# A two-model transformer kernel: GpSimd makes the output weights' remainders, and half of the attention rows are transposed during the last heads

## The chip, the cores and the metric

One Trainium2 chip, one core of it (NeuronCore). The metric is the device time of one launch in microseconds (us), the median of several executions. Engines: TensorE (PE) multiplies and transposes matrices, VectorE (DVE) and ScalarE (ACT) work on rows, GpSimd (POOL) is a third engine for rows and for gathers, SyncE (SP) issues the loads.

## The reference

256 rows of 1024 go first through two layers of a first model (attention, pooling, then an expert layer that gathers rows of two tables), then through four layers of a second one, and it is these four that the change touches. Cut to what matters:

```python
for i in range(4):                       # mixers: diff, moba, swa, diff
    a = rms_norm_2(h, attn_norm_g[i])
    h = h + mixer(a)                     # in-projection, attention, @ w_out
    h = h + sqrelu_mlp(rms_norm_2(h, mlp_norm_g[i]), mlp_w_up[i], mlp_w_down[i])

# inside diff_attention: 8 heads of 128 columns, each from two score matrices
p = softmax(s); p = p[:, :, 0] - lam * p[:, :, 1]
o = einsum('bhqk,bkhe->bqhe', p, v)
o = rms_norm_2(o, sub_g) * (1.0 - lambda_init)   # a norm per row and head
return o.reshape(B, S, H * DIFF_V_DIM) @ w_out
```

The moba and swa mixers have 16 heads of 64 columns and no norm per head.

## The kernel before, in words

All of it is written by hand: each engine has its own program, and semaphores are the only tie between them, so the order of the source is the order on each engine. 256 rows are NT = 2 tiles of 128.

**Matrix products in the last layers.** A product is made in three passes of reduced-precision matmuls (`three`, L773): high part by high part, remainder by high part, high part by remainder. A weight block of 1024 x 512 (a unit) is loaded by SP into one of two ring slots; ACT writes the high part of each of its four pieces (`high_at`, L1495, the instruction is L1502), and DVE the remainder, raw minus high (`low_at`, L1702, instruction L1706, 128x1024). SP loads unit u only when the remainders of unit u - 2 are made. The left operand is treated alike: PE transposes a group of four 128x128 blocks into a psum bank (`tr_group`, L712), ACT copies it to `xT_high` (`xT_high`, L1519; instructions L1523 without and L1526 with gains), DVE makes `xT_low` (`xT_low`, L1746; L1751 and L1755). `linear2` (L1122) then multiplies piece by piece; piece p needs the remainders of weight piece p and the p-th group of the left operand.

**Attention** (`attention`, one function per engine: PE L809, ACT L1325, DVE L1772) is a software pipeline over steps i = 0 to nsub + 3, nsub = 16. In step i, PE makes scores i (L826), transposes the probabilities of a head (L836) and multiplies an older head with the values (`values`, L848, L858). ACT takes exponentials (L1350) and copies transposed probabilities (L1332). DVE adds the mask to the scores (L1784), takes reciprocals of the sums (L1829) and copies finished heads, scaled, to `tokb` (`heads`, L1820). With the diff mixer two score matrices make one head: DVE combines them (`probs`, L1836 and L1842), and it sums each head's squares (`head_squares`, L1809).

**The end of attention and the output projection**, the place of the change. The high pieces of the first output unit (o0) are made by ACT within attention, in steps 5, 7, 9, 12 (diff), 5 to 8 (moba) or 13, 15, 16, 17 (swa). Their remainders are made by DVE in steps 16 to 18 (`after`, L2339), between the copies of the last heads. Then, once all heads are copied, the diff mixer takes means and reciprocals of the squares (L2363, L2364), ACT takes the square root (L1572; its table is loaded at L1570), and DVE scales both row tiles, 128x1024 each (L2370). For every mixer DVE then signals `tok_ready`, PE transposes groups 0 and 1 of `tokb` into psT, ACT and DVE split them, and `linear2` of o0 begins; groups 2 and 3 are transposed after its pieces 0 and 1.

**GpSimd** has nothing to do in the last four layers. In the two first layers it makes one remainder in four (L2429), which shows what such an instruction takes there.

## Time and profile before

| | us |
|---|---|
| median of 3 runs (3406.3 to 3417.52) | 3413.79 |
| the profiled execution's own time | 3393.41 |
| its span | 3391.3 |
| PE busy in the span | 2414.8 |
| DVE busy | 2118.6 |
| POOL busy | 1014.6 |
| ACT busy | 937.3 |

The four last layers begin at about 2127 us. There PE is busy in nine tenths of nearly every slice, DVE in five or six tenths, ACT in four or five, POOL in none. The profile names the line of kernel.py with L, and PEld is the load of a matmul's stationary operand. Rows give start and duration in us, the engine, line and operation, what was written and read, and in brackets how long the engine sat idle before and what released it. "x8" are eight like instructions merged in one row.

### The profile page before, as it was taken

To read this page: it belongs to the slowest core of one execution; us is meant where nothing else is said; L and a number is where in the kernel's file an instruction comes from. 1 tells how busy PE (TensorE), PEld (TensorE's weight loads), DVE (VectorE), ACT (ScalarE), POOL (GpSimd) and SP (SyncE) were. 2 spreads that over 40 slices of the span, in tenths; PEclk is the share of its full clock that TensorE was granted. 3 is DMA by queue.
4 is the path that set the end of the run, shared out by engine and by line. 5 is a ranking of instruction groups with operands and counts; after the bars stand their busy time and mean duration, and the time that the engine had idled before them with its cause. 6 is when DMAs were issued, how large, how long until landed. Compare 5 with 4: busy or idle time off the path is not lost.

```text
span 3391.3 us, 35250 instructions
## 1 busy us (share of the span) xinstructions
PE 2414.8 (71%) x12383; PEld 1718.0 (51%) x12383; DVE 2118.6 (62%) x4448; ACT 937.3 (28%) x1486; POOL 1014.6 (30%) x1044
## 2 busy tenths in 40 slices
PE   4996455444433998444545533889999999999898
PEld 3755222122101865221212200669888987997797
DVE  6965765666654975766656664565555556556654
ACT  2411110011101510101100100554455445545543
POOL 0202656666664200566666665000000000000000
PEclk9998776676766998666677755989999998999899
DMA  8764999999998872999998999525543542555243
GB/s 317 283 225 152 390 372 356 385 384 344 351 380 321 297 273 82 362 396 366 379 376 343 343 370 374 180 92 176 196 149 125 187 147 100 183 191 174 100 177 132
DMA packets 311815, 892.92 MB, mean 263 GB/s; under 512 B 22424, under 2 KB 31616, under 8 KB 311552
## 3 DMA queue, kind: packets, MB, share of 16 engines
q0 software_dynamic: 147456, 536.94, 41.1%
q1 hardware_dynamic: 164224, 354.32, 29.4%
q8 instruction: 68, 1.11, 0.1%
q14 instruction: 67, 0.55, 0.0%
HBM read 890.13 MB, written 1.05 MB: 263 GB/s over the span
## 4 chain that ended last, share of the span: by engine, by line
PE 50%; issue 14%; DVE 11%; POOL 10%; another core or an unknown queue 8%; DMA 4%; ACT 2%; SPq 0%; DVEq 0%; POOLq 0%; ACTq 0%; PEld 0%
PE lin L776 8%; PE lin L777 8%; PE lin L778 8%; PE psS L1020 4%; POOL proj L2445 4%; PE lin L1064 3%; PE lin L746 3%; POOL ring L2458 3%; DVE proj L2145 2%; POOL vbuf L2458 2%; PE psT L778 2%; PE psT L777 2%; PE psS L777 2%; PE psS L778 2%
## 5 line engine op out<-in xcount | busy, mean ns | idle before, releaser
L2145 DVE CUSTOM_DVE_ANT_0 proj<-proj,psT 128x1024 f32<-128x1024 f32 x512 | 608.2, 1219 | 228.8 <-DMA proj<-in_expert_u,eidx 145.6
L1706 DVE TENSOR_TENSOR weights_split<-ring,weights_split 128x1024 fp32r<-128x1024 f32 (+1 forms) x376 | 450.7, 1208 | 375.9 <-ACT weights_split L1502 373.0
L2445 POOL DMA_INDIRECT proj<-in_expert_u,eidx x512 | 483.5, 944 | 506.1 <-DVEq L2119 318.1
L1502 ACT ACTIVATE weights_split<-ring 128x1024 fp32r<-128x1024 f32 (+1 forms) x376 | 391.5, 1046 | 467.5 <-PE lin L778 291.4
L1064 PE MATMUL lin<-ring,rowb 128*32 128x512 f32 x896 | 205.0, 813 | 254.9 <-DMA pr<-in_expert_v,pT 103.6
L1064 PE MATMUL lin<-vbuf,rowb 128*32 128x512 f32 x1024 | 214.4, 830 | 195.4 <-issue 100.5
L776 PE MATMUL lin<-weights_split,xT_high 128*128 128x512 f32 (+1 forms) x736 | 297.0, 404 | 11.3 <-DVE xT_low L1755 5.2
L2458 POOL DMA_INDIRECT vbuf<-in_expert_v,pT x256 | 240.9, 941 | 165.1 <-issue 75.6
L778 PE MATMUL lin<-weights_split,xT_high 128*128 128x512 f32 (+1 forms) x736 | 288.9, 392 | 0.0
L1020 PE MATMUL psS<-xT,ring 128*128 128x256 f32 x1024 | 260.7, 414 | 31.1 <-issue 24.9
L2458 POOL DMA_INDIRECT ring<-in_expert_v,pT x224 | 215.3, 961 | 190.1 <-remote 72.5
L1020 PEld LDWEIGHTS psS<-xT,ring 128*128 128x128 f32 x1024 | 210.4, 209 | 104.7 <-issue 69.6
L1445 ACT ACTIVATE gel<-hdot 128x16 f32<-128x16 f32 x32 | 6.9, 216 | 839.8 <-remote 311.9
L1064 PEld LDWEIGHTS lin<-ring,rowb 128*32 128x32 f32 x896 | 37.0, 131 | 381.3 <-issue 198.7
L1064 PEld LDWEIGHTS lin<-vbuf,rowb 128*32 128x32 f32 x1024 | 42.2, 139 | 322.7 <-issue 320.1
L776 PE MATMUL lin<-weights_split,act_split 128*128 128x512 f32 x512 | 200.1, 391 | 0.0
L777 PE MATMUL lin<-weights_split,act_split 128*128 128x512 f32 x512 | 199.5, 390 | 0.0
L778 PE MATMUL lin<-weights_split,act_split 128*128 128x512 f32 x512 | 199.2, 389 | 0.0
L777 PE MATMUL lin<-weights_split,xT_low 128*128 128x512 f32 (+1 forms) x480 | 187.0, 390 | 0.0
L1051 PE MATMUL psS<-const,pT 128*128 128x16 f32 x64 | 16.6, 337 | 238.9 <-DVE pT L2132 135.6
L1430 ACT ACTIVATE sm<-psS 128x512 f32<-128x512 f32 x32 | 19.1, 597 | 550.2 <-remote 277.8
L776 PEld LDWEIGHTS lin<-weights_split,xT_high 128*128 128x128 f32 x736 | 143.3, 195 | 45.1 <-issue 9.4
(279 smaller groups left out, 4950.9 us busy)
## 6 DMA issues: line engine op xcount, KB each, us to landing
ring<-in_mlp_w_up SPq DMA_DIRECT2D x32, 2048.0 KB
ring<-in_mlp_w_down SPq DMA_DIRECT2D x32, 2048.0 KB
ring<-in_w_in SPq DMA_DIRECT2D x16, 2048.0 KB, 16.3
ring<-in_w_query SPq DMA_DIRECT2D x16, 2048.0 KB
vbuf<-in_ada_w SPq DMA_DIRECT2D x12, 2048.0 KB, 11.9
ring<-in_diff_w_in SPq DMA_DIRECT2D x12, 2048.0 KB, 13.1
ring<-in_ada_w SPq DMA_DIRECT2D x8, 2048.0 KB, 15.1
ring<-in_moba_w_in SPq DMA_DIRECT2D x6, 2048.0 KB
```

The costliest lines, as they stand in the source:

```text
L746: mm = pe.matmul(lin[:, pair + t, :], lhs[:, k, t * P:(t + 1) * P], rhs[:, k, :], start=(k == 0), stop=(k == kc - 1))
L776: pe.matmul(out_ap, lhs[0], rhs[0], start=first, stop=False, skip_group_check=True)
L777: pe.matmul(out_ap, lhs[1], rhs[0], start=False, stop=False, skip_group_check=True)
L778: return pe.matmul(out_ap, lhs[0], rhs[1], start=False, stop=last, skip_group_check=True)
L1020: mm = pe.matmul(psS[:, 1, (b % 2) * S:(b % 2 + 1) * S], ring[:, j, k, b * P:(b + 1) * P], xT[:, k, :], start=(k == 0), stop=(k == KC - 1))
L1064: mm = pe.matmul(lin[32 * b:32 * b + 32, 2 * half + t, :], wst[:, cb % 2, 4 * b + s, :], vrow(SETROWS * s + b)[:, half * 512:(half + 1) * ...
L1430: act.activation(qTx[:, lo:lo + 2, :].rearrange("p a s -> p (a s)"), psS[:, 1, :], ACT.Copy).then_inc(q_used, 1)
L1502: act.activation(part(p, 0, kind, w), raw_piece(slot, p, kind, w), ACT.Copy).then_inc(hi_ready, 1)
L1706: dve.tensor_tensor(part(p, 1, kind, w), raw_piece(slot, p, kind, w), part(p, 0, kind, w).bitcast(F32), ALU.subtract).then_inc(lo_ready, 1)
L2145: dve.tensor_tensor_reduce(ubuf[:, n % GB, :], ubuf[:, n % GB, :], x_row, 1.0, 0.0, ALU.mult, ALU.add, hdot[:, cb, k:k + 1]).then_inc(h_re ...
L2445: pool.indirect_dma_start(out=ubuf[:, (16 * cb + k) % GB, :], out_offset=None, in_=table["u"], in_offset=bass.IndirectOffsetOnAxis(ap=eidx ...
L2458: pool.indirect_dma_start(out=vrow(SETROWS * s + b), out_offset=None, in_=table["v"], in_offset=bass.IndirectOffsetOnAxis(ap=eidxT[:, cb % ...
```

## The change

Four things, in the last four layers only.

1. The four remainders of unit o0 are made by GpSimd, in each of the four layers (16 instructions), each as soon as ACT's high piece is there. DVE makes none of them any more.
2. PE transposes groups 0 and 1 (heads 0 to 3 with diff, 0 to 7 with moba and swa) in step 18 of attention, before it multiplies the last heads, into banks 2 and 3 of `lin`. It waits for `tok_ready` there, which DVE now signals twice per layer, the first time at the start of step 17.
3. With diff, mean, reciprocal, square root and scaling are done per half of the heads: the first half's statistics in step 16 and its scaling at the start of step 17; the second half's scaling after the split of groups 0 and 1. ACT loads the square root's table in step 16, ahead of its last copy.
4. ACT and DVE split groups 0 and 1 from `lin` right after attention.

```diff
@@ PE, attention(..., early=None) @@
                         mm.then_inc(pt_done, 1)
+                    if early is not None and i == m.nsub + 2:
+                        early()
                     o = m.head_at(i, 3)
@@ PE, per layer @@
+                def first_heads():
+                    pe.wait_ge(tok_ready, 2 * i + 1)
+                    pe.wait_ge(lin_used, C.lin)
+                    for g in range(2):
+                        for n, (b, t) in enumerate((b, t) for b in range(2) for t in range(NT)):
+                            mm = pe.transpose(lin[:, 2 + g, n * P:(n + 1) * P], tokb[:, t, (2 * g + b) * P:(2 * g + b + 1) * P], ident)
+                        mm.then_inc(tr_done, 1)
+                        C.tr += 1
...
                 pe.wait_ge(pt_copied, C.out)
                 pe.wait_ge(pv_used, C.out)
-                pe.wait_ge(tok_ready, i + 1)
-                tr1 = C.tr
+                tr1 = C.tr - 2
...
                 def later_heads(p):
+                    if p == 0:
+                        pe.wait_ge(tok_ready, 2 * i + 2)
                     if p < 2:
                         head_group(2 + p)
-                head_group(0)
-                head_group(1)
                 linear2(UC, tr1, later_heads)
@@ ACT, per layer @@
+                def head_rstd(h0, done):
+                    act.wait_ge(hn_sq, done)
+                    act.activation(st[:, 44:60].rearrange("p (t h) -> p t h", t=NT)[:, :, h0:h0 + 4],
+                                   st[:, 24:40].rearrange("p (t h) -> p t h", t=NT)[:, :, h0:h0 + 4], ACT.Sqrt).then_inc(hn_rs, 1)
                 def beside(i):
+                    if m is DIFF and i == m.nsub:
+                        act.activation(st[:, 62:63], cst("iota")[:, 1:2], ACT.Sqrt)
+                        head_rstd(0, 2 * slot + 1)
...
                 attention(C, m, beside)
+                gains = None if m is not DIFF else pcol[:, 64 + 8 * slot:72 + 8 * slot]
+                xT_high(C, gains, 0, 4, [lin[:, 2, :], lin[:, 3, :]])
                 if m is DIFF:
-                    act.activation(st[:, 62:63], cst("iota")[:, 1:2], ACT.Sqrt)
-                    act.wait_ge(hn_sq, i // 3 + 1)
-                    act.activation(st[:, 44:60], st[:, 24:40], ACT.Sqrt).then_inc(hn_rs, 1)
-                xT_high(C, None if m is not DIFF else pcol[:, 64 + 8 * (i // 3):72 + 8 * (i // 3)])
+                    head_rstd(4, 2 * slot + 2)
+                xT_high(C, gains, 4, KC)
@@ DVE, per layer @@
-                def after(n):
-                    if n < 3:
-                        low_at(o_slot, q0, "flat", D, range(n, n + 1 + (n == 2)))
...
                 def beside(n):
+                    if m is DIFF and n == m.nsub:
+                        half_stats(0)
+                    if n == m.nsub + 1:
+                        if m is DIFF:
+                            half_scale(0, 2 * slot + 1)
+                        else:
+                            dve.wait_ge(pv_used, C.out + m.nout // 2)
+                        dve.sem_inc(tok_ready, 1)
...
                 dve.wait_ge(pv_used, C.out)
                 if m is DIFF:
                     head_squares(m.nout - 1)
...
-                    link(ins)
-                dve.sem_inc(tok_ready, 1)
-                xT_low(C, None if m is not DIFF else pcol[:, 64 + 8 * slot:72 + 8 * slot])
+                    half_stats(4)
+                    xT_low(C, gains, 0, 4, halves)
+                    half_scale(4, 2 * slot + 2)
+                    dve.sem_inc(tok_ready, 1)
+                else:
+                    dve.sem_inc(tok_ready, 1)
+                    xT_low(C, gains, 0, 4, halves)
+                xT_low(C, gains, 4, KC)
+                dve.wait_ge(lo_ready, q0 + NPC)
@@ GpSimd, new, for each mixer @@
+                for p in range(NPC):
+                    pool.wait_ge(hi_ready, q0 + p + 1)
+                    pool.tensor_tensor(part(p, 1, "flat", D), raw_piece(o_slot, p, "flat", D), part(p, 0, "flat", D).bitcast(F32),
+                                       ALU.subtract).then_inc(lo_ready, 1)
```

`half_stats(h0)` takes mean and reciprocal of the four heads from h0 on, `half_scale(h0, done)` waits for the square root and scales them, two instructions of 128x512.

How the order moves. First PE at the end of the first diff layer's attention, before:

```order
L836 MATMUL psT<-const,pr 128x128 [waits probs_transposed_copied,probs_ready]
L836 MATMUL psT<-const,pr 128x128 x2
L858 MATMUL lin<-proj,pT 128x128 [waits heads_copied,probs_transposed_copied]
L858 MATMUL lin<-proj,pT 128x128 x2
L712 MATMUL psT<-const,tokb 128x128 [waits attention_rows_ready,transposes_copied,heads_copied,probs_transposed_copied]
L712 MATMUL psT<-const,tokb 128x128 x3
L712 MATMUL psT<-const,tokb 128x128 [waits transposes_copied]
L712 MATMUL psT<-const,tokb 128x128 x3
L776 MATMUL lin<-weights_split,xT_high 128x512 [waits piece_low_ready,linear_copied,transposes_copied]
```

and after (L860 is the old L858):

```order
L836 MATMUL psT<-const,pr 128x128 [waits probs_transposed_copied,probs_ready]
L836 MATMUL psT<-const,pr 128x128 x2
L1180 MATMUL lin<-const,tokb 128x128 [waits linear_copied,attention_rows_ready]
L1180 MATMUL lin<-const,tokb 128x128 x7
L860 MATMUL lin<-proj,pT 128x128 [waits heads_copied,probs_transposed_copied]
L860 MATMUL lin<-proj,pT 128x128 x2
L776 MATMUL lin<-weights_split,xT_high 128x512 [waits linear_copied,transposes_copied,piece_low_ready,heads_copied,probs_transposed_copied]
```

The eight transposes stand ahead of the last head's value product, with a wait of their own. Then DVE in the same place, from the seventh head's probabilities on, before:

```order
L1842 SCALAR_TENSOR_TENSOR pr<-proj,st 128x256
L1706 TENSOR_TENSOR weights_split<-ring,weights_split 128x1024
L1809 ISA xn,st<-tokb 128x128
L1820 TENSOR_TENSOR tokb<-lin,gel 128x2x128
L1706 TENSOR_TENSOR weights_split<-ring,weights_split 128x1024 x3
L1820 TENSOR_TENSOR tokb<-lin,gel 128x2x128
L2363 TENSOR_SCALAR st<-st 128x16
L2364 RECIPROCAL st<-st 128x16
L2370 TENSOR_TENSOR tokb<-tokb,st 128x1024 x2
L1755 SCALAR_TENSOR_TENSOR xT_low<-psT,pcol,xT_high 128x256 x8
```

and after (L1866, L1833, L1844, L1779 are the old L1842, L1809, L1820, L1755):

```order
L1866 SCALAR_TENSOR_TENSOR pr<-proj,st 128x256
L2376 TENSOR_TENSOR tokb<-tokb,st 128x512 x2
L1833 ISA xn,st<-tokb 128x128
L1844 TENSOR_TENSOR tokb<-lin,gel 128x2x128
L1844 TENSOR_TENSOR tokb<-lin,gel 128x2x128
L2366 TENSOR_SCALAR st<-st 128x2x4
L2367 RECIPROCAL st<-st 128x2x4
L1779 SCALAR_TENSOR_TENSOR xT_low<-lin,pcol,xT_high 128x256 x4
L2376 TENSOR_TENSOR tokb<-tokb,st 128x512 x2
L1779 SCALAR_TENSOR_TENSOR xT_low<-psT,pcol,xT_high 128x256 x4
```

The four remainders are gone from between the head copies, and the scaling is cut in two. (Between these rows stand more of the squares, L1809 and L1833.)

## Rows read from the trace of the kernel before

**Rows 1.** The page, busy time of the engines.
```profile
PE 2414.8 (71%) x12383; PEld 1718.0 (51%) x12383; DVE 2118.6 (62%) x4448; ACT 937.3 (28%) x1486; POOL 1014.6 (30%) x1044
```
**Rows 2.** Timeline, all engines, end of the first diff attention (start, duration, engine).
```profile
2237.93 1.22 DVE L1706 TENSOR_TENSOR weights_split<-ring,weights_split 128x1024 fp32r<-128x1024 f32 x1
...
2239.37 1.28 ACT L1570 ACT_TABLE_LOAD   x1
...
2239.40 1.65 PE L858 MATMUL lin<-proj,pT 128*128 128x128 f32 x6 [0.58 <-ACT pT L1332]
...
2239.83 3.49 DVE L1706 TENSOR_TENSOR weights_split<-ring,weights_split 128x1024 fp32r<-128x1024 f32 x3
...
2243.65 0.42 DVE L1820 TENSOR_TENSOR tokb<-lin,gel 128x256 f32<-128x256 f32 x1
...
2245.20 0.22 ACT L1572 ACTIVATE st<-st 128x16 f32<-128x16 f32 x1 [4.34 <-DVEq L2365]
2245.45 2.36 DVE L2370 TENSOR_TENSOR tokb<-tokb,st 128x1024 f32<-128x1024 f32 x2 [0.34 <-ACT st L1572]
...
2248.13 1.94 PE L712 MATMUL psT<-const,tokb 128*128 128x128 f32 x8 [7.08 <-DVEq L2372]
...
2250.13 1.73 DVE L1755 SCALAR_TENSOR_TENSOR xT_low<-psT,pcol,xT_high 128x256 fp32r<-128x256 f32 x4 [2.31 <-ACT xT_high L1526]
...
2251.06 0.80 PE L776 MATMUL lin<-weights_split,xT_high 128*128 128x512 f32 x1 [0.99 <-DVE xT_low L1755]
```
**Rows 3.** Timeline, PE, end of the second diff attention.
```profile
3172.58 0.80 PE L776 MATMUL lin<-weights_split,xT_high 128*128 128x512 f32 x1 [0.99 <-DVE xT_low L1755]
```
**Rows 4.** Timelines of PE and of DVE, end of the moba attention.
```profile
2558.98 1.62 PE L858 MATMUL lin<-proj,pT 128*128 128x64 f32 x12
...
2565.95 0.80 PE L776 MATMUL lin<-weights_split,xT_high 128*128 128x512 f32 x1 [0.56 <-DVE xT_low L1751]
...
2562.86 0.28 DVE L1820 TENSOR_TENSOR tokb<-lin,gel 128x128 f32<-128x128 f32 x1
2565.20 0.69 DVE L1751 TENSOR_TENSOR xT_low<-psT,xT_high 128x512 fp32r<-128x512 f32 x1 [2.06 <-ACT xT_high L1523]
```
**Rows 5.** Windows of 1 us, moba: length, PE busy, granted clock, DMA share, GB/s.
```profile
2562.00:2563.00 1.00, 0.00 (x0) 0.77 0.00 0
...
2569.00:2570.00 1.00, 1.00 (x5) 0.82 0.98 369
```
**Rows 6.** Timeline, PE, end of the swa attention.
```profile
2849.12 1.45 PE L858 MATMUL lin<-proj,pT 128*128 128x64 f32 x6 [0.44 <-ACT pT L1332]
...
2854.29 0.79 PE L776 MATMUL lin<-weights_split,xT_high 128*128 128x512 f32 x1 [0.56 <-DVE xT_low L1751]
```
**Rows 7.** Timelines of POOL and of DVE, first layer, one GpSimd remainder.
```profile
57.11 2.35 POOL L2429 TENSOR_TENSOR weights_split<-ring,weights_split 128x1024 fp32r<-128x1024 f32 x1 [56.65 <-ACT weights_split L1378]
...
57.06 0.99 DVE L1858 TENSOR_SCALAR pr<-psT,aff,modc 128x256 f32<-128x256 f32 x2 [0.16 <-DVE pr L1858]
58.21 1.81 DVE L1868 TENSOR_TENSOR first_xT_low<-pr,xT_high 128x512 fp32r<-128x512 f32 x1 [0.15 <-DVE pr L1858]
```
**Rows 8.** Timelines of ACT and DVE, first diff attention, around the high pieces of o0.
```profile
2218.75 1.04 ACT L1502 ACTIVATE weights_split<-ring 128x1024 fp32r<-128x1024 f32 x1
...
2223.45 0.29 DVE L1784 CUSTOM_DVE_ANT_0 sm<-psS,const 128x128 f32<-128x128 f32 x1 [0.98 <-PE psS L826]
...
2222.02 1.04 ACT L1502 ACTIVATE weights_split<-ring 128x1024 fp32r<-128x1024 f32 x1
2224.01 0.29 DVE L1809 CUSTOM_DVE_ANT_0 xn<-tokb 128x128 f32<-128x128 f32 x1
...
2227.03 0.18 DVE L1829 RECIPROCAL gel<-hdot 128x4 f32<-128x4 f32 x1 [1.22 <-ACT rope_t L1350]
...
2230.16 1.05 ACT L1502 ACTIVATE weights_split<-ring 128x1024 fp32r<-128x1024 f32 x1
...
2231.99 0.29 DVE L1809 CUSTOM_DVE_ANT_0 xn<-tokb 128x128 f32<-128x128 f32 x1
```

More of the change, by code:

```diff
@@ L807, in gqa_columns, with attention @@
                 C.tr += 1
-            def attention(C, m, v_piece=None, late=None, v_at=DENSE_AT):
+            def attention(C, m, v_piece=None, late=None, v_at=DENSE_AT, early=None):
                 if v_piece is not None:
@@ L2337, in _, with half_stats, half_scale @@
                 o_slot, _ = C.next_slot()
-                def after(n):
-                    if n < 3:
-                        low_at(o_slot, q0, "flat", D, range(n, n + 1 + (n == 2)))
-                def beside(n):
+                def half_stats(h0):
+                    means = st[:, 24:40].rearrange("p (t h) -> p t h", t=NT)[:, :, h0:h0 + 4]
+                    link(dve.tensor_scalar(means, means, 1.0 / P, EPS, ALU.mult, ALU.add))
+                    link(dve.reciprocal(means, means))
+                    dve.sem_inc(hn_sq, 1)
+                def half_scale(h0, done):
+                    dve.wait_ge(hn_rs, done)
+                    for t in range(NT):
+                        rows = tokb[:, t, h0 * P:(h0 + 4) * P].rearrange("p (h d) -> p h d", d=P)
+                        rstd = st[:, 44 + 8 * t + h0:48 + 8 * t + h0].rearrange("p (h d) -> p h d", d=1).to_broadcast([P, 4, P])
+                        ins = dve.tensor_tensor(rows, rows, rstd, ALU.mult)
+                    link(ins)
+                def beside(n):
+                    if m is DIFF and n == m.nsub:
[6 more added lines that the diff above has]
+                        dve.sem_inc(tok_ready, 1)
+                    if m is not SWA:
+                        return
                     if n in (1, 2):
@@ L2357, in beside @@
                         swa_columns(C, m, 6)
-                attention(C, m, after, beside if m is SWA else None)
+                attention(C, m, None, beside)
                 dve.wait_ge(pv_used, C.out)
+                gains = None if m is not DIFF else pcol[:, 64 + 8 * slot:72 + 8 * slot]
+                halves = [lin[:, 2, :], lin[:, 3, :]]
                 if m is DIFF:
                     head_squares(m.nout - 1)
-                    link(dve.tensor_scalar(st[:, 24:40], st[:, 24:40], 1.0 / P, EPS, ALU.mult, ALU.add))
-                    link(dve.reciprocal(st[:, 24:40], st[:, 24:40]))
-                    dve.sem_inc(hn_sq, 1)
-                    dve.wait_ge(hn_rs, slot + 1)
-                    for t in range(NT):
-                        rows = tokb[:, t, :].rearrange("p (h d) -> p h d", d=P)
-                        rstd = st[:, 44 + 8 * t:52 + 8 * t].rearrange("p (h d) -> p h d", d=1).to_broadcast([P, 8, P])
-                        ins = dve.tensor_tensor(rows, rows, rstd, ALU.mult)
-                    link(ins)
-                dve.sem_inc(tok_ready, 1)
-                xT_low(C, None if m is not DIFF else pcol[:, 64 + 8 * slot:72 + 8 * slot])
+                    half_stats(4)
[7 more added lines that the diff above has]
+                dve.wait_ge(lo_ready, q0 + NPC)
                 low(C)
```

30 lines of the change are left out of this document (21 added, 9 removed).

## The prediction, made before the changed kernel was timed

> **What bounds the kernel now.** I began with the busy line: PE leads [rows 1], and in the last four layers it is busy nearly all the time. The question is thus where PE stands still there. The timeline shows it at the end of each attention. In the first diff layer PE ends its last value product at 2241.05 (2239.40 + 1.65), stands for 7.08, transposes for 1.94, waits 0.99 more and starts the output projection at 2251.06 [rows 2]. What it waits for is DVE: one weight remainder at 2237.93, three more from 2239.83 to 2243.32, only then the copy of the last head at 2243.65, the statistics, ACT's square root at 2245.20 and 2.36 of scaling. The second diff layer does the same 921.5 later [rows 3]. The moba and swa layers have no norm, and their gaps are shorter: from 2560.60 to 2565.95 [rows 4] and from 2850.57 to 2854.29 [rows 6]. From the projection on, PE is the bound, so what the projection starts earlier should reach the end of the kernel.
>
> **What GpSimd's remainders cost.** One takes 2.35 us on GpSimd [rows 7] against 1.22 on DVE [rows 2]. ACT's last high piece is done at 2231.21 (2230.16 + 1.05) [rows 8], so the four remainders are ready long before the projection, and their own time costs nothing on GpSimd. The cost is on DVE. While GpSimd ran from 57.11 to 59.46, a DVE instruction with two inputs in SBUF started at 58.21 and ended at 60.02, 0.56 after GpSimd: it was held. The pair that reads psT beside it took its 0.99 undisturbed [rows 7]. So I hold every DVE instruction with two SBUF inputs (squares L1809, combining L1836 and L1842) until GpSimd is done, and let pass those that read psum (scores L1784, head copies L1820, the split of the left operand).
>
> The trace has no row of an instruction with one input in psum and one in SBUF beside GpSimd, and scores, head copies and splits are of that kind. The Trainium skill (GPSIMD Engine Reference, section Specifications) names as contending only DVE instructions in a 2-port mode or with two SBUF inputs. By that rule these pass and the sum below stands; were they held too, the slower rival below would come nearer.
>
> The diff layers, piece by piece. Piece 0 falls in a DVE pause. Piece 1 is there at 2219.79 (2218.75 + 1.04); GpSimd is done by about 2222.4, and DVE is under 1 us late, which the 0.98 pause before 2223.45 takes up. Piece 2 comes at 2223.06; GpSimd runs to about 2225.6 and holds the squares of 2224.01 for 1.6, of which the 1.22 pause before 2227.03 and PE's own waits take nearly all. Piece 3 comes at 2231.21, GpSimd holds to about 2233.8, and the squares of 2231.99 wait 1.8 [rows 8]. Here DVE has hardly a pause (about 0.2 per head), so **1.6 us is added** to each diff attention. From below the cost is 0 (all in pauses), from above four times 2.35, 9.4 a layer (none in a pause). I take 1.6, since the rows show the pauses. In moba DVE has no two-input instruction in attention but scores and copies, in swa only a sum of 128x4 whose delay is under 1 us, beside the path: 0 for both.
>
> **The sum, diff.** The seventh pair of probabilities ends at 2237.93 + 1.6 = 2239.5. ACT's table load (1.28, now without cover from DVE's remainder), the touch of 0.2 and the square root of 0.22 start with the last exponential, some 1.15 ahead of that, so the root of the first half is there at 2240.05. Scaling half the heads is half of 2.36: 2241.25, and PE may transpose, 1.94: 2243.2. **The last value product stands behind this new wait**: 1.65 more, 2244.85, against 2241.05 before. Then head copy to square root, 1.55 as before (2243.65 to 2245.20): 2246.4; the split of group 0, begun 0.93 ahead of the first matmul as before (2250.13 to 2251.06): 2247.35. Gain **3.7** per layer, 7.4 for both. The second half's scaling (1.2) and transposes lie under piece 0's matmuls, and the weights' remainders are there. Unit 8's load starts earlier, which helps nobody: ACT takes it up after PE has used o1.
>
> **Moba.** PE goes on from 2560.60 with eight transposes more, 0.97 at full clock (half of 1.94): 2561.6. Copy 0.28, split 0.69, hand-overs 0.2: 2562.75, against 2565.95. **3.2.** The granted clock fell to half only at about 2562.5, 1.9 after PE had stopped, and stayed there to about 2569.4 [rows 5], so that 3.4 us of the projection ran at half clock. The new pause is 1.15, so I expect the clock to stay at 2.4 GHz: 1.7 more, **4.9** in all.
>
> **Swa.** The last value product waits for ACT's copy at 2849.12 either way. The transposes fill the pauses ahead of it, so I give it full clock and 0.9: 2850.0, then the same 1.15: 2851.15 against 2854.29. **3.1.** Whether the clock then stays up as well is open; I don't count it.
>
> Sum: 7.4 + 4.9 + 3.1 = **15.4 us**. From the profiled execution's 3393.41 that gives 3378.0. The median of the runs is 20.4 above it and is what I predict for: 3413.79 - 15.4 = **3398.4**. About 0.3%, 10 us, is what a measurement of this kernel can tell from no change.
>
> **Rivals.**
> - *The clock gains more.* In swa it may stay at full as in moba, and in the diff layers it may rise sooner, since PE is busy from 2241.25 on. Some 2.3 in swa and 1 in each diff layer: 19.7, 3394.1. For it: the pauses shrink everywhere. Against: in the diff layers about 2.5 us of pause remain. Chance 0.25.
> - *DVE is held in more places.* If the pauses don't take up pieces 1 and 2, each diff layer loses 3 more and moba some 2: 15.4 - 8 = 7.4, 3406.4. For it: DVE, ACT and PE hand over to each other in every step, so a late score can delay the next exponential. Chance 0.12.
> - *The time saved is lost at the next wait.* The new start of o0 meets the high and low pieces of o1, which ACT and DVE can only make after groups 2 and 3. If those set the pace with the full clock, half the gain goes: 7, 3406.8. Against: two pieces of o0, 5.5 us of matmuls, cover about 3.5 of ACT and DVE. Chance 0.08.
> - *Slower: GpSimd's sixteen instructions hold DVE in full.* If every DVE instruction that touches SBUF is held, scores and copies with it, each GpSimd instruction costs 2.35 on a path without pauses: 16 x 2.35 = 37.6, against gains of 2 x 5.3 + 4.9 + 3.1 = 18.6. That is 19 slower, 3432.8. It decides from 18.6 / 16 = 1.2 per instruction on. For it: DVE has almost no pause in diff. Against: the undisturbed psum pair, and pauses of over 1 us per step in moba. Chance 0.05.
>
> **How the numbers follow.** The forecast has 0.50. Faster by over 0.3% are the forecast and the first rival, 0.75. Within it are the second and third, 0.20. The slower one has 0.05. The range takes the first rival with 2 us more for its end, 3392, and goes up over the second and third to 3409: it leaves out the slower case and a little on both sides.
>
> **What the new profile would show.** GpSimd's sixteen subtractions of about 2.4; DVE's squares held for about 1.8 after the last high piece of each diff layer, scores and copies not; the transposes at about 2241.3 with the last value product behind them; PE's first L776 of the projection at 2247.4 in the first diff layer (offset by nothing that comes before it), and 3.1 to 3.2 sooner after the last scores in moba and swa; in moba a granted clock of 1.00 throughout. I am wrong if scores or splits are stretched next to GpSimd, if PE's gap ahead of the projection is not shorter by some 3 us in each layer, or if the stretch from the projection to the layer's end grows by what was gained.

## The result: 16.6 us faster, a hair below the range

| | before | changed |
|---|---|---|
| median of 11 runs each, us | 3408.34 | 3391.77 |
| lowest to highest | 3402.74 to 3423.7 | 3383.24 to 3403.9 |
| profiled execution's own time | 3393.41 | 3384.06 |
| its span | 3391.3 | 3382.0 |

The ratio is 0.9948 with a 95% interval of 0.9932 to 0.9963: faster by 0.5%. (All ratios compare fast executions; two of the experiments had one execution at a lower granted clock each, 0.59 and 0.69, of 4024 and 3606 us, which are left out.) I forecast 15.4 us on 3413.79, a ratio of 0.9955, and that lies in the interval. The time itself, 3391.77, lies 0.2 below my range (3392 to 3409), because the median of before, taken over 11 runs instead of 3, is 5.5 lower. The gain of the medians is 1.2 more than forecast.

The page of the changed kernel, busy time by engine and the group of the new instructions:

```profile
PE 2430.0 (72%) x12383; PEld 1715.8 (51%) x12383; DVE 2110.4 (62%) x4440; ACT 936.7 (28%) x1488; POOL 1044.5 (31%) x1060
...
L2540 POOL TENSOR_TENSOR weights_split<-ring,weights_split 128x1024 fp32r<-128x1024 f32 x16 | 37.9, 2376 | 998.9 <-ACT weights_split L1513 998.9
```

Against [rows 1] PE has the same 12383 instructions; DVE has 16 remainders fewer and, from the halves, eight small instructions more (4440 against 4448); POOL has the sixteen new ones, 2.38 us each. None of these totals says where the gain is. For that I cut the last four layers at the same instructions in both traces: first scores, end of the last value product, first matmul of the output projection (o0), first matmul of the MLP. T0 is the start of the first weight product (L776) of the last four layers. Attention is counted from the first scores to the end of the last value product.

| us | diff 1 | moba | swa | diff 2 | sum |
|---|---|---|---|---|---|
| before: attention | 37.45 | 39.56 | 43.60 | 37.45 | |
| pause ahead of o0 | 10.02 | 5.35 | 3.72 | 10.08 | |
| o0 to the MLP | 25.73 | 25.33 | 26.13 | 25.72 | |
| together | 73.20 | 70.24 | 73.45 | 73.25 | 290.14 |
| changed: attention | 41.55 | 40.25 | 43.04 | 43.12 | |
| pause ahead of o0 | 2.68 | 1.39 | 1.40 | 2.69 | |
| o0 to the MLP | 26.12 | 25.33 | 23.74 | 25.33 | |
| together | 70.35 | 66.97 | 68.18 | 71.14 | 276.64 |

(The pause of before has the eight transposes in it; those of the changed kernel stand ahead of the last value product and count as attention.) The stages give 13.5 less; the MLPs are alike to 0.01. From T0 to the end it is 1251.4 before and 1238.8 after, 12.6 less. What lies ahead of T0, where nothing was changed, took 2139.85 and 2143.22.

The clock must be read beside these numbers. TensorE's granted clock is either 2.4 or 1.2 GHz, and a "fall" is a stretch at 1.2. One of 3.4 us costs some 1.6 where PE is busy throughout: in two runs of one kernel, below, the stretch from o0 to the MLP in moba took 23.72 without a fall and 25.32 with one.

The timeline of PE in the changed kernel, end of the first diff attention (start, duration, engine; in brackets the idle time before and what released it):

```profile
2240.80 0.90 PE L836 MATMUL psT<-const,pr 128*128 128x128 f32 x3 [2.39 <-DVE pr L1866]
2242.28 1.65 PE L860 MATMUL lin<-proj,pT 128*128 128x128 f32 x6 [0.58 <-ACT pT L1343]
2244.40 0.90 PE L836 MATMUL psT<-const,pr 128*128 128x128 f32 x3 [0.47 <-DVE pr L1866]
2246.15 1.97 PE L1180 MATMUL lin<-const,tokb 128*128 128x128 f32 x8 [0.85 <-DVEq L2387]
2247.91 1.49 PE L860 MATMUL lin<-proj,pT 128*128 128x128 f32 x6
2252.08 0.77 PE L776 MATMUL lin<-weights_split,xT_high 128*128 128x512 f32 x1 [2.68 <-issue]
```

The pause of 7.08 in [rows 2] is gone. The transposes (L1180) now wait 0.85, for the signal behind DVE's scaling, and the last value product stands behind them. The other side of it, DVE of the changed kernel in the same layer:

```profile
2224.14 2.52 DVE L1833 CUSTOM_DVE_ANT_0 xn<-tokb 128x128 f32<-128x128 f32 x1
...
2236.15 0.42 DVE L1808 CUSTOM_DVE_ANT_0 sm<-psS,const 128x256 f32<-128x256 f32 x1
...
2236.49 1.90 DVE L1833 CUSTOM_DVE_ANT_0 xn<-tokb 128x128 f32<-128x128 f32 x1
...
2243.60 0.75 DVE L1866 SCALAR_TENSOR_TENSOR pr<-proj,st 128x128 f32<-128x128 f32 x2
...
2244.74 1.29 DVE L2376 TENSOR_TENSOR tokb<-tokb,st 128x512 f32<-128x512 f32 x2 [0.40 <-ACT st L1575]
```

and POOL:

```profile
2218.03 2.38 POOL L2540 TENSOR_TENSOR weights_split<-ring,weights_split 128x1024 fp32r<-128x1024 f32 x1 [104.99 <-ACT weights_split L1513]
2224.11 2.40 POOL L2540 TENSOR_TENSOR weights_split<-ring,weights_split 128x1024 fp32r<-128x1024 f32 x1 [3.71 <-ACT weights_split L1513]
...
2235.80 2.44 POOL L2540 TENSOR_TENSOR weights_split<-ring,weights_split 128x1024 fp32r<-128x1024 f32 x1 [3.83 <-ACT weights_split L1513]
2540.37 9.31 POOL L2540 TENSOR_TENSOR weights_split<-ring,weights_split 128x1024 fp32r<-128x1024 f32 x4 [302.13 <-ACT weights_split L1513]
```

Two squares (L1833) take 2.52 and 1.90, where their fellows take 0.29. They end at 2226.66 and 2238.39, GpSimd at 2226.51 and 2238.24: each was held until GpSimd was done, as forecast. The third remainder held something too, a combining factor of 128x2 with its inputs in SBUF (usually 0.22), and in swa a sum of 128x4 (usually 0.16) was held. Each of the two ends 0.02 after a GpSimd instruction (2231.97, and 2845.56 for the first of the three merged below), so a small instruction waits like a large one:

```profile
2229.61 2.36 POOL L2540 TENSOR_TENSOR weights_split<-ring,weights_split 128x1024 fp32r<-128x1024 f32 x1 [3.09 <-ACT weights_split L1513]
2231.51 0.48 DVE L1860 SCALAR_TENSOR_TENSOR st<-gel,st,hdot 128x2 f32<-128x2 f32 x1
...
2843.19 7.06 POOL L2540 TENSOR_TENSOR weights_split<-ring,weights_split 128x1024 fp32r<-128x1024 f32 x3 [1.53 <-ACT weights_split L1513]
2844.59 0.99 DVE L1852 TENSOR_TENSOR hdot<-hdot,actw 128x4 f32<-128x4 f32 x1 [2.07 <-ACT actw L1364]
```

The score row of 2236.15, which reads psum and SBUF and ran beside the same remainder as the second square, took its usual 0.42. Over the whole program no score row was stretched, which one line of the view by source line shows (minimum, median, maximum in ns):

```profile
L1808 DVE CUSTOM_DVE_ANT_0 sm<-psS,const x160: 275/419/426, 167.1 to 3152.5; 128x256 f32<-128x256 f32 x96, 128x128 f32<-128x128 f32 x64
```

Nor were the other kinds: in moba, where GpSimd ran from 2540.37 to 2549.68, a reciprocal with one SBUF input and a head copy that reads psum; in swa two splits of the left operand (psum and SBUF, 0.69 each, two merged below), beside the remainder that ran from 2847.89 to 2850.25.

```profile
2542.25 0.17 DVE L1853 RECIPROCAL gel<-hdot 128x4 f32<-128x4 f32 x1
2542.46 0.29 DVE L1844 TENSOR_TENSOR tokb<-lin,gel 128x128 f32<-128x128 f32 x1
...
2848.61 1.29 DVE L1775 TENSOR_TENSOR xT_low<-lin,xT_high 128x512 fp32r<-128x512 f32 x2 [0.16 <-DVE tokb L1844]
```

Two things on the hold stood already in the first layers of the kernel before, and the forecast did not use them:

```profile
86.01 1.22 DVE L1850 TENSOR_TENSOR weights_split<-ring,weights_split 128x1024 fp32r<-128x1024 f32 x1
86.06 3.42 POOL L2429 TENSOR_TENSOR weights_split<-ring,weights_split 128x1024 fp32r<-128x1024 f32 x1 [9.23 <-ACT weights_split L1378]
87.14 2.63 DVE L1874 TENSOR_SCALAR rope_t<-vbuf,cact 128x512 f32<-128x512 f32 x1
```

GpSimd can be the one that waits: started 0.05 behind a DVE remainder, it took 3.42 instead of 2.35. And L1874, which reads one tensor from SBUF and one value per row, took 2.63 where its median is 0.48. So one SBUF tensor is not always safe; which property of L1874 makes it wait, no run here separates.

Moba and swa, PE of the changed kernel:

```profile
2561.25 1.45 PE L860 MATMUL lin<-proj,pT 128*128 128x64 f32 x12
2564.09 0.51 PE L776 MATMUL lin<-weights_split,xT_high 128*128 128x512 f32 x1 [1.39 <-issue]
...
2565.25 0.63 PE L776 MATMUL lin<-weights_split,xT_high 128*128 128x512 f32 x1
...
2849.52 0.47 PE L776 MATMUL lin<-weights_split,xT_high 128*128 128x512 f32 x1 [1.39 <-issue]
...
2850.29 0.39 PE L776 MATMUL lin<-weights_split,xT_high 128*128 128x512 f32 x1
```

The pause is the same 1.39 in both. The matmuls behind it take 0.63 in moba and 0.39 in swa, and the windows of 1 us (length, PE busy, granted clock, DMA share, GB/s) show the granted clock, first moba, then swa:

```profile
2564.00:2565.00 1.00, 0.91 (x3) 0.69 0.00 0
2565.00:2566.00 1.00, 1.00 (x4) 0.50 0.00 0
...
2567.00:2568.00 1.00, 1.00 (x4) 0.60 0.00 0
...
2849.00:2850.00 1.00, 0.48 (x2) 1.00 0.00 0
2850.00:2851.00 1.00, 1.00 (x6) 1.00 0.06 16
```

In moba it fell to half all the same; in swa it stayed at 2.4 GHz.

### The profile page after: what moved, and what is told of

Its sections match the earlier page's. It is cut to its first block, busy times and chain, and to the rows that moved or that the text cites. A ratio compares the mean times of both kernels' runs of the same rounds, so it can differ in the third digit from the quotient of the medians.

```text
span 3382.0 us, 35276 instructions
## 1 busy us (share of the span) xinstructions
PE 2430.0 (72%) x12383; PEld 1715.8 (51%) x12383; DVE 2110.4 (62%) x4440; ACT 936.7 (28%) x1488; POOL 1044.5 (31%) x1060
## 4 chain that ended last, share of the span: by engine, by line
PE 49%; issue 14%; DVE 14%; POOL 9%; another core or an unknown queue 8%; DMA 4%; ACT 2%; SPq 0%; DVEq 0%; POOLq 0%; ACTq 0%; PEld 0%
PE lin L776 8%; PE lin L778 8%; PE lin L777 8%; DVE proj L2169 4%; POOL proj L2491 4%; PE psS L1022 4%; PE lin L746 3%; POOL ring L2504 2%; PE lin L1066 2%; DMA proj<-in_expert_u,eidx 2%; POOL vbuf L2504 2%; PE psT L778 2%; PE psT L777 2%; PE psS L777 2%
## 5 line engine op out<-in xcount | busy, mean ns | idle before, releaser
L1729 DVE TENSOR_TENSOR weights_split<-ring,weights_split 128x1024 fp32r<-128x1024 f32 (+1 forms) x360 | 431.6, 1207 | 376.1 <-ACT weights_split L1513 373.5
L1066 PE MATMUL lin<-ring,rowb 128*32 128x512 f32 x896 | 228.4, 835 | 284.8 <-issue 151.6
L2540 POOL TENSOR_TENSOR weights_split<-ring,weights_split 128x1024 fp32r<-128x1024 f32 x16 | 37.9, 2376 | 998.9 <-ACT weights_split L1513 998.9
L776 PE MATMUL lin<-weights_split,xT_high 128*128 128x512 f32 (+1 forms) x736 | 294.7, 400 | 16.7 <-issue 8.2
L776 PE MATMUL lin<-weights_split,act_split 128*128 128x512 f32 x512 | 200.1, 391 | 0.0
L776 PEld LDWEIGHTS lin<-weights_split,xT_high 128*128 128x128 f32 x736 | 142.2, 193 | 51.0 <-issue 18.7
```

The lines of the kernel that those rows point to most:

```text
L776: pe.matmul(out_ap, lhs[0], rhs[0], start=first, stop=False, skip_group_check=True)
L1066: mm = pe.matmul(lin[32 * b:32 * b + 32, 2 * half + t, :], wst[:, cb % 2, 4 * b + s, :], vrow(SETROWS * s + b)[:, half * 512:(half + 1) * ...
L1729: dve.tensor_tensor(part(p, 1, kind, w), raw_piece(slot, p, kind, w), part(p, 0, kind, w).bitcast(F32), ALU.subtract).then_inc(lo_ready, 1)
L2540: pool.tensor_tensor(part(p, 1, "flat", D), raw_piece(o_slot, p, "flat", D), part(p, 0, "flat", D).bitcast(F32), ALU.subtract).then_inc(lo ...
```

## The experiments

Twelve runs follow, of ten kernels: eight new ones (one of them twice), the changed kernel twice more, and the kernel before once more. Times are compared with the kernel before on the same chip; its median differed by chip (3408, 3395, 3265, 3265 and 3406), and nearly all of that difference lies ahead of T0 (2134 to 2148 us on the slower chips, 2008 to 2014 on the faster ones; in the changed kernel's profiles 129 of 133 us). The MLPs take the same on every chip, to 0.02 us, so the stages can be compared across chips.

### The changed kernel again

No edit.

> The changed kernel once more, to see which of its stages repeat. Theory (the gain lies at the ends of the four attentions, the rest is spread): from the first matmul of the last layers to the end some 12.7 us less than before again (1238.8 against 1251.5 in the profile), while the start of the last layers moves by several us from one execution to the next. Rival (the change also shortens the first two layers): the last layers begin earlier than before's 2139.85 in this profile too, by 3 us or more. Where the granted clock falls behind each attention may differ from the first profile by up to 2 us a layer.

Measured: 3378.86 against 3395.45, ratio 0.9954 (0.9936 to 0.9972). The stages gave 70.26, 66.96, 68.12 and 71.13, within 0.1 of those above, falls of the clock included; from T0 to the end it took 1238.5. T0 itself came at 2137.14, 2.7 earlier than before's and 6.1 earlier than in the first profile of the same program, so nothing says that the change reaches the first layers.

### Only GpSimd's remainders, nothing else of the change

```diff
@@ the kernel before: DVE, per layer @@
-                attention(C, m, after, beside if m is SWA else None)
+                attention(C, m, None, beside if m is SWA else None)
...
+                dve.wait_ge(lo_ready, q0 + NPC)
@@ GpSimd: the loop of the change @@
```

> Only part 1: GpSimd makes o0's remainders; scaling and transposes as before. Theory (GpSimd holds DVE's instructions with two SBUF inputs): each diff layer loses about 2 to 3 us in attention and gets back 2.6 at the end of it, since the last head copy no longer waits behind remainders: 0 within 1; moba 2 us faster, swa 0.6; in all 3 us faster than before. Rival (GpSimd costs DVE nothing): each diff layer 2.5 us faster, in all 8 us. Rival (the whole gain comes from taking the remainders off DVE): 12 us or more.

Measured: ratio 0.9988 (0.9973 to 1.0002). The stages: diff 73.67 and 74.82 (0.5 and 1.6 more than before), moba 67.63 (2.6 less), swa 71.57 (1.9 less); together 2.45 less. In the first diff layer the pause ahead of o0 shrank from 10.02 to 7.45, and attention grew from 37.45 to 39.57. The second has a fall of the clock early in attention, worth 1.5. Up to o0 the first diff layer gained 0.4 and lost 0.9 behind it, by the clock. So in diff the hold takes back what the absent remainders give, and GpSimd pays only in moba (2.7 in the pause) and swa (0.6 in the pause, 0.2 in attention, the rest by the clock).

### All but GpSimd's remainders

```diff
@@ the changed kernel: DVE, per layer @@
+                def after(n):
+                    if n < 3:
+                        low_at(o_slot, q0, "flat", D, range(n, n + 1 + (n == 2)))
...
-                attention(C, m, None, beside)
+                attention(C, m, after, beside)
@@ GpSimd: the loop is taken out @@
```

> All but part 1: halves and early transposes as in the changed kernel, the remainders on DVE in steps 16 to 18 as before. Theory: the early transposes and halves carry most of the gain: diff 3 us each, moba 2, swa 2, in all 10 us faster than before, about 3 slower than the changed kernel. Rival (the two parts only work together, since DVE is full in the last steps): under 5 us faster than before.

Measured: ratio 0.9956 (0.9938 to 0.9973). Stages 69.90, 68.74, 70.88 and 69.74, together 10.9 less than before. The diff layers are better than with GpSimd (70.35 and 71.14): attention 40.18 instead of 41.55, the pause 4.05 instead of 2.68, 44.2 either way up to o0 in the first layer. What is left of the difference is the clock. Moba and swa are 1.8 and 2.7 worse: their pauses are 3.19 and 2.53 instead of 1.39, and the other 1.6 of swa is a fall of the clock behind the pause. The medians can't tell this kernel from the changed one (0.9956 and 0.9954); the stages can.

### The diff layers' last two remainders after attention

```diff
@@ the changed kernel: GpSimd @@
-            for m in MIXERS2:
+            for i, m in enumerate(MIXERS2):
...
                     pool.wait_ge(hi_ready, q0 + p + 1)
+                    if m is DIFF and p == 2:
+                        pool.wait_ge(tok_ready, 2 * i + 2)
```

> The changed kernel, but in the diff layers GpSimd waits with pieces 2 and 3 until DVE has scaled the second half of the rows. Theory (piece 3 holds DVE's squares for 1.6 to 1.9 us where DVE has no pause): the two stretched squares after the last high piece are back at 0.29, and each diff attention ends 2 us sooner than in the changed kernel, 4 us in all. Rival (the hold is taken up by waits elsewhere): no change. Rival (the first MLP unit's load, which now starts some 20 us later, comes too late): up to 5 us slower behind o1.

Measured: ratio 0.9937 (0.9918 to 0.9956). The diff stages were 67.37 and 68.58, 3.0 and 2.6 less than in the changed kernel, and attention of the first was 39.38 instead of 41.55. The hold is gone altogether: the last probabilities were done 34.44 after the first scores, against 36.50 in the changed kernel and 34.42 before, although the second remainder still held a square for 2.2. The rest of the 3.0 is the clock behind the pause. POOL shows where the two pieces went, well behind the last squares and still ahead of their use:

```profile
2242.98 4.71 POOL L2542 TENSOR_TENSOR weights_split<-ring,weights_split 128x1024 fp32r<-128x1024 f32 x2 [25.38 <-DVEq L2414]
```

Swa, which this edit doesn't touch, was 3.1 longer (71.25): its attention was 44.54 instead of 43.04, and o0 to the MLP 25.31 instead of 23.74, both by the clock: it was at half for 10.2 us at the start of attention instead of 6.8, and again for 3.4 behind the pause.

### The diff layers' transposes behind the last value product

```diff
@@ the changed kernel: PE, attention @@
-                    if early is not None and i == m.nsub + 2:
+                    if early is not None and m is not DIFF and i == m.nsub + 2:
                         early()
...
                         values(C, m, o)
+                    if early is not None and m is DIFF and i == m.nsub + 3:
+                        early()
```

> The changed kernel, but in the diff layers PE makes the eight transposes behind the last value product, not ahead of it. Theory (in diff the last value product waits for the scaled first half, and its 2 us of transposes at half clock, for nothing): the last value product starts 1.9 us sooner, the transposes end when it would have, and the projection starts 1.7 us sooner in each diff layer. Rival (the split of group 0 then waits for the transposes instead): 0.5 us or less sooner, or later.

Measured: ratio 0.9923 (0.9904 to 0.9942). Its PE timeline, first diff layer:

```profile
2109.50 1.65 PE L862 MATMUL lin<-proj,pT 128*128 128x128 f32 x6 [0.58 <-ACT pT L1345]
2110.94 1.91 PE L1182 MATMUL lin<-const,tokb 128*128 128x128 f32 x8
2114.00 0.76 PE L776 MATMUL lin<-weights_split,xT_high 128*128 128x512 f32 x1 [1.14 <-issue]
```

The transposes no longer wait, and the last head's copy and squares on DVE run beside them. From the first scores to the first matmul of o0 it took 42.20 instead of 44.23: 2.0. The second diff layer took 42.20 as well, instead of 45.81, of which 1.5 was the fall of the clock. Run again beside the changed kernel, below, it gave the same ratio.

### Twice the work on GpSimd

In the diff layers GpSimd makes every remainder twice.

```diff
@@ the changed kernel: GpSimd @@
+                    if m is DIFF:
+                        pool.tensor_tensor(part(p, 1, "flat", D), raw_piece(o_slot, p, "flat", D), part(p, 0, "flat", D).bitcast(F32),
+                                           ALU.subtract).then_inc(pchain, 1)
...
+                        pool.wait_ge(pchain, twice[0])
```

> The changed kernel, but in the diff layers GpSimd makes each remainder twice before it reports it. Theory (GpSimd holds DVE's two-input instructions as long as it runs): each piece holds for up to 2.4 us more, of which pauses take some, so each diff attention ends 4 to 8 us later, and squares of about 4 us or two stretched ones per piece are seen; scores and head copies keep 0.29, 0.42 and 0.42. Rival (only the start of a GpSimd instruction costs DVE something): under 1 us a layer. Rival (instructions with one input in psum are held too): scores are stretched.

Measured: ratio 0.998 (0.997 to 0.9989). Attention in the diff layers was 45.14 and 45.66, 3.6 and 2.5 more than in the changed kernel; in the first layer below the 4 to 8 that I expected. The second figure compares with an attention that lost 1.5 to the clock, which this one did not; without that it is 4.1. From the first scores to the last probabilities the first layer took 40.09, against 36.50 with one dose and 34.42 with none. That is far from the nothing of the rival. And the kind of instruction that is held is the same (view by source line: squares, combining factors, scores):

```profile
L1833 DVE CUSTOM_DVE_ANT_0 xn<-tokb x32: 279/290/2490, 2089.4 to 3035.4; 128x128 f32<-128x128 f32 x32
...
L1860 DVE SCALAR_TENSOR_TENSOR st<-gel,st,hdot x16: 220/236/1287, 2076.9 to 3028.6; 128x2 f32<-128x2 f32 x16
...
L1808 DVE CUSTOM_DVE_ANT_0 sm<-psS,const x160: 275/419/426, 168.4 to 3026.0; 128x256 f32<-128x256 f32 x96, 128x128 f32<-128x128 f32 x64
```

The scores stayed at 426 at most with twice the GpSimd time beside them.

### Late pieces and late transposes together

The edits of the two kernels above, a wait ahead of piece 2 and the transposes last.

> Late pieces 2 and 3 together with the transposes behind the last value product, both in the diff layers alone. Theory: the two gains add, about 2.8 and 1.7 us a layer, since the one ends the hold in the last steps and the other takes a wait off the chain behind them: 9 us in all against the changed kernel, some 22 against the kernel before, less what the granted clock takes back in one layer or another (up to 3 us). Rival (they overlap, since with late pieces the first half is scaled sooner and the last value product waits less): 6 us in all.

Measured: ratio 0.9916 (0.9899 to 0.9932). Diff 64.17 and 66.11, attention 37.31 and 37.67: the two gains add up nearly (3.8 up to o0 in the first layer, against 2.0 and 2.2). But swa was 72.79, its attention 46.08 where it is 41.58 with the transposes alone, again by the clock.

### Which of the two late pieces counts

As the last kernel, with the wait ahead of piece 3 alone (`p == 3`).

> Transposes behind the last value product, and of the diff layers' remainders only piece 3 late. Theory: the hold in the last steps, the one that DVE has no pause for, is that of piece 3, so each diff attention ends as early as with pieces 2 and 3 late (37.3 to 37.7 us from the first scores to the last value product, against 39.4 with the transposes alone): stage 65.5 to 66 without clock loss. Rival: piece 2's hold counts as much, then 38.5. Where the granted clock falls in swa can't be foreseen: 66.7 or 72.8 were seen.

Measured: ratio 0.9924 (0.9906 to 0.9942). Attention of the first diff layer was 37.55, against 39.36 with the transposes last alone (39.68 in its second run, below) and 37.31 with both pieces late. So piece 3's hold is worth 1.8 to 2.1 and piece 2's 0.2, which is the 0.26 for which it holds the small combining factor. The second diff layer had 39.07, of which 1.5 is a fall of the clock.

### GpSimd for moba and swa only

```diff
@@ the changed kernel: DVE @@
-                attention(C, m, None, beside)
+                def after(n):
...
+                attention(C, m, after if m is DIFF else None, beside)
@@ GpSimd @@
-                for p in range(NPC):
+                for p in range(NPC if m is not DIFF else 0):
```

> The changed kernel, but in the two diff layers the remainders are back on DVE, in steps 16 to 18; moba and swa keep GpSimd. Theory (in diff GpSimd's holds cost more than the remainders did on DVE, once halves and early transposes are in; in moba and swa they cost nothing): each diff stage from attention to the first MLP matmul takes the 69.8 us that it took with all remainders on DVE, against 70.3 and 71.1 in the changed kernel, moba stays at 67.0, swa at 68 to 71 by the granted clock: 0 to 2 us faster than the changed kernel. Rival (GpSimd is worth having in every layer): 3 us slower in all.

Measured: ratio 0.9954 (0.9936 to 0.9973). Diff 70.12 and 71.82, against 69.58 and 71.86 of the changed kernel on the same chip; moba and swa as with GpSimd. No square was held now, the longest of 32 taking 294 ns:

```profile
L1833 DVE CUSTOM_DVE_ANT_0 xn<-tokb x32: 282/286/294, 2090.2 to 3027.9; 128x128 f32<-128x128 f32 x32
```

Up to o0 the two diff layers took 44.20 and 45.98, against 44.23 and 45.83. In the diff layers it thus makes no difference who makes the remainders; my 69.8 for each stage held for neither, by the clock.

### Two repeats on one chip

The kernel with the transposes last, and the changed kernel, side by side.

> The kernel with the transposes behind the last value product once more, on the same chip as the changed kernel. Theory (stages repeat to about 0.1 us, the clock's falls included, since they follow from what the program does): 265.4 us in the four stages again, 11 less than the changed kernel. Rival (the falls are chance): stages differ by 1.5 us or more from the first time.

> The changed kernel a third time, on the same chip as the three others. Theory: 276.5 us in the four stages, 13.5 less than before, and a ratio to before of 0.995 to 0.996 whatever the chip. Rival: its stages change with the chip as the first layers do.

Measured: ratios 0.9924 (0.991 to 0.9937) and 0.995 (0.9937 to 0.9964), medians 3241.11 and 3249.27. The better order is 8 us ahead of the change; its two diff stages are 3.3 and 5.9 shorter, of which 1.7 and, apart from the fall in attention, some 2.1 lie ahead of o0; the rest is the clock. The changed kernel's profile gave 1235.4 from T0 to the end, 16.0 less than before's 1251.4: here the clock in swa did not fall in the in-projection (32.10 instead of 33.70) and fell for only 3.4 us instead of 6.8 in attention (41.56 instead of 43.05).

The first and the second run of the *same* kernel with the transposes last differ in the stages: moba 65.37 and 67.01, swa 66.69 and 68.16 with an in-projection of 32.06 and 33.70; the four stages gave 265.4 and 267.4. So the stages do not repeat to 0.1, and the rival, 1.5 or more of difference, came true. The two runs were on different chips, so whether the chip or chance moved the falls stays open. In moba the pause was 1.39 both times; the first time the clock stayed up behind it (o0 to the MLP 23.72), the second time it fell (25.32). The windows of the first run, moba:

```profile
2424.00:2425.00 1.00, 0.00 (x0) 1.00 0.00 0
2425.00:2426.00 1.00, 0.92 (x4) 1.00 0.00 0
2426.00:2427.00 1.00, 1.00 (x7) 1.00 0.00 0
```

### The kernel before, against itself

> The kernel before, profiled once more. Theory (the first two layers differ by chip, the last four don't, but for the places where the granted clock falls): 1251.5 us from the first matmul of the last layers to the end, within 3; the four stages from first scores to first MLP matmul 73.2, 70.2, 73.5, 73.3, each within 0.2 or off by 1.5 where the clock differs. Rival (the last layers go with the chip as well): stages differ in parts where TensorE's clock is the same.

Measured: 3402.03 against 3406.13, ratio 0.9987 (0.9974 to 0.9999). From T0 to the end it took 1251.3, as forecast. The same program came out 0.13% apart, with an interval that just misses 1. The stages gave 73.24, 70.25, 73.03 and 73.49, 290.0 in all. So a ratio of 0.998 or 0.999 says little by itself here, and 0.3% as the bound of what can be told was fair.

## Why the prediction came out as it did

- **The bound** was right. PE's pauses ahead of the output projection were where time could be had, and what the projection starts earlier reaches the end of the kernel: the MLPs behind it are alike to 0.01.
- **The price on GpSimd**, 2.35 each and under cover: 2.38 measured. It was read from one row, and that row is the shortest of 16 in the first layers (2.35 to 3.49, median 2.75), where GpSimd can be the one that waits (the 3.42 above). In the last layers it never had to for longer than 0.1.
- **The hold** was right in kind and nearly in size. Squares and two small instructions with two SBUF inputs wait for GpSimd; scores, head copies, splits and reciprocals don't. The rule of the Trainium skill (GPSIMD Engine Reference, section Specifications), that instructions with two SBUF inputs contend with GpSimd, agrees with every row of the last four layers that is shown here. I had put 1.6 us into each diff attention; up to the end of the last probabilities it was 2.1 in the first diff layer (34.42 before, 36.50 after). By places I was less right. The second remainder (2224.11) held a square for 2.2, where I had under 1, but the pauses took up all of it: with only that hold left, the last probabilities came at 34.44. ACT's third high piece came 2.2 later for it, and so the third remainder met no square. It held the combining factor for 0.26, which costs 0.2 to 0.3, where I had expected 1.6, taken up. The fourth cost 1.5 to 1.8 up to there, as I had it.
- **The diff chain behind the last probabilities** was right almost to the instruction: from there to the first matmul of the projection I had 7.85 and it took 7.82 (13.13 before; like the forecast these two count from 0.09 ahead of the end of the row, where the next instruction may start). Gain up to o0 in the first diff layer: 3.24, forecast 3.7, the difference being the hold. The second gave 1.72. There 1.5 more went to a fall of the clock within attention, over the last matmuls of the value projection (0.63 each from 3121.5 to 3124, where 0.40 is usual). It came at the same place in all three profiles of the changed kernel, and in those with only GpSimd's remainders, with piece 3 late and with GpSimd for moba and swa only; not in the others. Why is open.
- **Moba**: forecast 3.2 for the start, measured 3.27. The 1.7 for the clock **failed**: "I expect the clock to stay at 2.4 GHz". From o0 to the MLP it took 25.33 as before, so this term gave 0.0: the clock fell 0.3 after the pause of 1.39 and stayed at half for 3.4 us, as long as before behind the start of o0. The step that failed is the reasoning from the length of the pause, for the same length ended both ways.
- **Swa**: forecast 3.1, measured 2.88 (47.32 to 44.44); and the clock, which I had left out, stayed up and gave 2.39 more. The two clock terms exchanged places, and the sum hid it.
- **The sum.** Of 15.4 the first profile shows 12.6 (3.24 + 1.72 + 3.27 + 2.88 = 11.1 up to o0, 2.4 behind it, 0.9 lost in the first in-projection, whose start was at half clock for 4.7 us instead of 2.8), the profile on the faster chip 16.0, the medians 16.6 and, repeated on two other chips, 16.6 and 16.2. Falls of the clock account for nearly all the difference between the two profiles (3.1 of 3.4: 1.6 in the in-projection of swa and 1.5 in its attention); how often each fall comes in the unprofiled runs can't be seen, and that part of the medians stays open. The two profiles on slower chips show 12.6 and 12.9 where the medians show 16.6, so some 4 of the measured gain is seen in no stage, and that the medians came within 1.2 of the forecast is in part luck.
- **The range** failed by 0.2, and the step is the baseline, the 3413.79 of "3413.79 - 15.4": I set it about a median of 3 runs that spread over 11 us, and gave that spread no place. The median of 11 was 3408.34, 5.5 lower; from 3413.79 the measured gain of 16.6 would have ended at 3397.2, inside. In ratios the forecast holds; in microseconds the range should have reached some 5 lower on that account alone.
- **The rivals.** DVE held in more places: hardly, in diff 0.5 more than forecast, in swa one sum for 0.83. Gain lost at the next wait: no, o0 to the MLP grew by at most 0.4. Held in full: no, by the score rows and by the doubled dose, which cost 6.1 (7.7 without the fall of the clock that it was spared) where eight more instructions at 2.35 would have cost 19. The clock gains more: half true, swa yes, moba and diff no.
- **What I missed** is in the change's own order. "The last value product stands behind this new wait": I wrote it and priced it, but not as a loss that could be had back. It costs 2.0 per diff layer. And I credited GpSimd in diff without asking what the change would be without it: nothing, as the kernels without it show. The gain in the diff layers comes from the halves and the early transposes; GpSimd's share is 1.8 in moba and 1.1 in swa, with 1.6 more in swa from a fall of the clock that may or may not be due to it.
- **What was not tried**: the transposes last in moba and swa, and the same question put to DVE. In the changed kernel DVE stands idle for 1.82 ahead of the last head's copy at 2249.44, while ACT writes the high parts of groups 0 and 1 (from 2247.31), but it makes their low parts, which the projection waits for, only from 2251.00, behind that copy, its squares and the statistics.

The best versions are the change with the diff layers' transposes last (0.9923 and 0.9924), and with piece 3 late as well (0.9924) or pieces 2 and 3 (0.9916). The three can't be told apart by their medians; a fall of the clock in swa took 5 to 6 us from the last in its profile. The first is the simplest.

## What to carry to other kernels

Work that GpSimd has idle time for is free there, but each such instruction can hold DVE until it is done, when an instruction with two SBUF inputs, however small, comes up beside it. What that costs is the part that no pause of DVE takes up (here 0, 0.2 to 0.3 and 1.5 to 1.8 for three holds of 2.2, 0.26 and 1.6): place it beside instructions that read psum, or behind the last of the others. When part of an end is pulled forward on an in-order engine, ask what now stands behind its wait; in the diff layers the transposes, which wait for scaled rows, belonged behind the last product, not ahead of it. And forecast a gain as a ratio, or give the baseline's own spread a place in the range.

## What the runs showed of the hardware that I had not expected

- A pause of the same length ended both ways. After 1.39 us without matmuls PE ran on at 2.4 GHz in swa, and in moba fell to 1.2 GHz 0.3 later; in moba of one and the same kernel, on two chips, it once stayed and once fell. Such a pause says nothing certain of the clock behind it.
- Falls of the clock move. Edits in the diff layers alone changed the swa layer's stage between 66.7 and 72.8 us, more than most of the edits were worth. A gain must be read in its own stage.
- The same kernel differed by 4% between chips, nearly all of it in the two first layers, and by 0.13% against itself on one chip.
- An instruction of 128x2 or 128x4 with two SBUF inputs waits for GpSimd like a large one (0.48 and 0.99 us instead of 0.22 and 0.16; up to 1.29 with the doubled dose), and in the first layers the 128x512 tensor_scalar with one SBUF tensor waited as well (2.63 instead of 0.48).
